# Expert weights fetched with rows p and p + 128 in one partition instead of two neighbouring rows

## The chip, the cores and the metric

The kernel runs on one core of one Trainium2 chip. The metric is the device time of one execution in microseconds (us). A core has five engines with instruction queues of their own: TensorE (PE; its weight loads are listed apart as PEld), VectorE (DVE), ScalarE (ACT), GpSimd (POOL) and SyncE (SP), which here only issues transfers. 16 DMA engines move the data of all queues.

## The reference, cut to what matters

Two transformer blocks over 256 tokens of 1,024 features, in float32. The first mixes tokens and then retrieves single-neuron experts, 128 per token, out of a table of 16,384 rows. The second has a recurrent mixer, an attention and then a mixture of 32 experts, each of which is a 1,024 x 2,048 matrix for gate and up and a 1,024 x 1,024 matrix down:

```python
def expert_block(args):
    tok, e = args
    xb = h[tok]
    gu = xb @ w_gate_up[e] + b_gate_up[e]
    gate = jnp.minimum(gu[:, :D_FF], SWIGLU_LIMIT)
    up = jnp.clip(gu[:, D_FF:], -SWIGLU_LIMIT, SWIGLU_LIMIT)
    act = (up + 1.0) * gate * jax.nn.sigmoid(SWIGLU_ALPHA * gate)
    return act @ w_down[e] + b_down[e]
```

A router picks 4 experts per token. All 32 experts are needed, so 32 x 12.58 MB = 402.65 MB of weights are read once.

## The kernel before

SBUF holds a ring of 12 slots of 1,024 KB (8 KB in each of 128 partitions) and an arena that is laid out anew in each stage.

Stage one, to about 1,060 us. The weights of the dense layers come as a stream of 93 chunks, one slot each (SP, L639). `slot_of` says which slot a chunk takes: the first 48 go round the ring; the q chunks take `Q_SLOTS`, the keys and what follows take the slots of `FREE`, and the remaining seven slots (`G_SLOTS`) hold rows of the table of single-neuron experts, 256 gathers of 128 rows of 8 KB that GpSimd issues (L743). A chunk is issued when TensorE has counted `chunk_done` past the last user of its slot. Work of the second block is woven into the gathers; what is left of it is done after them, to the transposes of the residual at L2235 and the router at L2249.

Stage two, the 32 experts. A weight transfer ("pair") moves 2,048 KB: two k-chunks of 128 rows of `w_gate_up` (four pairs per expert), or four of `w_down` (two pairs). There are nine places: six are two slots of the ring each (`in_ring`), three lie in the arena. Transfer m goes to place m % 9. SP issues the first nine when the last users of their place are through, and each later one when the transfer nine before it is used up (L648, in `pair`). Slots 10 and 11, 5 and 6, 7 and 8, 3 and 4, 0 and 1 are neighbours; place 7 is slots 2 and 9.

With `(p i)` in the source's order, partition p holds rows 2p and 2p + 1 of the 256 rows of the pair. A k-chunk is then the even or the odd rows, so the other operand must have its features in that order too. The kernel gets this by reading every second column in the transposes (`front_turn`, L2310; L2235 for the router's input), by reading every fourth for the input of `w_down` (L2338), and by permuting the matching columns on the host (`paired`).

An expert on TensorE: 64 matmuls of gate and up (L2324), the gathering of the next expert's tokens (L2291), biases (L2302), transposes of the activation (L2338), of the next expert's input (L2310) and of the scatter matrix (L2344), 32 matmuls down (L2355), and 8 that add the result into the residual (L2367). TensorE waits in `pair(q)` for the landing of each weight pair.

Of the kernel before, what the change touches and what calls it, by code (L numbers as in the profile page):

```python
# [14 lines left out]
P = 128  # L15
D = 1024
T = 256
TT = T // P
KD = D // P
CW = 256  # L20
# [23 lines left out]
NE = 32  # L44
# [34 lines left out]
ADA_PARTS = (0, 1, 3, 4, 2, 5)  # L79
N_PARTS = len(ADA_PARTS)  # L80
# [41 lines left out]

Q_SLOTS = (0, 1, 2, 4, 0, 1, 2, 4)
FREE = (0, 1, 2, 4, 3)
G_SLOTS = tuple(sorted(set(range(SLOTS)) - set(FREE)))
GB, NF = len(G_SLOTS), len(FREE)
PICKS = TT * HK
# [130 lines left out]
def build(nc, xd, stream, colsd, matsd, rowsd, badad, expert_uv, w_gate_up, w_down, bias_moe, out):  # L260
    with ExitStack() as ctx:
# [8 lines left out]
        xres = sb("xres", [P, TT, D])  # L270
# [5 lines left out]
        ident = sb("ident", [P, P])  # L276
# [17 lines left out]
        psum = ctx.enter_context(nc.psum_tensor("psum", [P, 8, 512], F32))  # L294
# [121 lines left out]
        xs = area(6144, W2)  # L416
        xT = area(6656, 4, P)
        ag = area(7168, 512)
# [204 lines left out]
        @block.sync  # L623
        def _(sp):
            sp.dma_start(cols[:], colsd).then_inc(loaded_c, 16)
            for tt in range(TT):
                sp.dma_start(xres[:, tt, :], xd[tt * P:(tt + 1) * P, :]).then_inc(loaded_x[tt], 16)
            held = {}
            for n in LOADS:
                if C_MB + N_GATHER <= n < C_MB + N_GATHER + GB:  # L630
                    sp.wait_ge(v_done, PICKS - GB + (n - C_MB - N_GATHER) + 1)
                elif slot_of(n) in held:
                    sp.wait_ge(chunk_done, held[slot_of(n)] + 1)
                if n == C_MB + N_FIRST:
                    sp.wait_ge(v_done, PICKS - LEFT)
                held[slot_of(n)] = n
                kind = STREAM[n][:2]
                width = KD * LAST if kind == ("rw", N_RW - 1) else CHUNK
                sp.dma_start(slot(n)[:, 0:width], stream[ROW[kind], :, 0:width]).then_inc(landed[slot_of(n)], 16)  # L639

            def pair(e, q, at):

                if q < GU_PAIRS:
                    src = w_gate_up[e, q * 2 * P:(q + 1) * 2 * P, :].rearrange("(p i) c -> p i c", i=2)
                else:
                    r = (q - GU_PAIRS) * 4 * P
                    src = w_down[e, r:r + 4 * P, :].rearrange("(p i k) c -> p i (k c)", i=2, k=2)
                sp.dma_start(place(at), src).then_inc(pair_in(at)[0], 16)  # L648


            for m in range(PLACES):
                if m in in_ring:
                    sp.wait_ge(chunk_done, max(n for n in range(C_MOE) if slot_of(n) in in_ring[m]) + 1)
                elif m == 4:
                    sp.wait_ge(pv_mm, TT)
                    sp.wait_ge(yp_mm, TT)
                    sp.wait_ge(fg_mm, 4 * TT)
                elif m == 5:
                    sp.wait_ge(chunk_done, AT["o2", 0, TT - 1] + 1)
                else:  # L660
                    sp.wait_ge(chunk_done, AT["o2", N_O2 - 1, TT - 1] + 1)
                pair(m // E_PAIRS, m % E_PAIRS, m)

            for m in range(PLACES, AHEAD * E_PAIRS):
                sp.wait_ge(chunk_done, C_MOE + (m - PLACES + 1))
                pair(m // E_PAIRS, m % E_PAIRS, m % PLACES)
            with sp.Fori(0, (NE - AHEAD) // ROUND) as i:
                for k in range(ROUND * E_PAIRS):
                    m = AHEAD * E_PAIRS + k
                    sp.wait_ge(chunk_done, i * (ROUND * E_PAIRS) + (C_MOE + m - PLACES + 1))  # L670
                    pair(i * ROUND + m // E_PAIRS, m % E_PAIRS, m % PLACES)

            def experts(p):
                with sp.Fori(0, NE) as e:
                    for q in range(E_PAIRS):
                        sp.wait_ge(chunk_done, (p * NE + e) * E_PAIRS + (C_MOE + q - E_PAIRS + 1))
                        pair(e, q, last_pass_place(q))

            further_passes(sp, experts)
            sp.wait_ge(out_ready, 1)  # L680
            for tt in range(TT):
                sp.dma_start(out[tt * P:(tt + 1) * P, :], xres[:, tt, :]).then_inc(stored, 16)
            sp.wait_ge(stored, 16 * TT)
# [1057 lines left out]
        def _(pe):  # L1741
# [264 lines left out]
            def mixer(tt):  # L2006
# [223 lines left out]
                for m in range(2):  # L2230
                    yield "tn%d" % m
                    pe.wait_ge(xn_ready[3], 2 * tt + m + 1)
                    for k in range(4 * m, 4 * m + 4):
                        at = k // 2 * 2 * P + k % 2
                        last = pe.transpose(psum[:, m, k % 4 * P:(k % 4 + 1) * P], xres[:, tt, at:at + 2 * P - 1:2], ident[:])  # L2235
                    last.then_inc(turned[3], 1)
                if tt:
                    pe.wait_ge(picks_ready, 1)
# [66 lines left out]
            def front_turn(f):  # L2305
                pe.wait_ge(xs_ready, f + 1)
                for j in range(4):

                    at = j // 2 * 2 * P + j % 2
                    last = pe.transpose(psum[:, 3, j * P:(j + 1) * P], xs[:, at:at + 2 * P - 1:2], ident[:])  # L2310
                last.then_inc(xt_mm, 1)

            def expert(it, f, pair):

                pe.wait_ge(xT_ready, f + 1)
                for kt in range(GU_CHUNKS):
                    if kt % 2 == 0:
                        both = pair(kt // 2)
                    w = both[:, kt % 2, :]
                    x = xT[:, kt % 4, CAP * (kt // 4):CAP * (kt // 4) + CAP]  # L2320
                    for gu in range(2):
                        for h in range(2):
                            at = gu * FF + h * 512
                            last = pe.matmul(psum[CAP * h:CAP * h + CAP, gu, :], x, w[:, at:at + 512],  # L2324
                                             start=False, stop=(kt == GU_CHUNKS - 1), skip_group_check=True)
                    if kt % 2 and kt < GU_CHUNKS - 1:
                        last.then_inc(chunk_done, 1)
                last.then_inc(gu_mm, 1)

                pe.wait_ge(sct_ready, it + 1)  # L2330
                front_gather(f + 1, frees=True)
                pe.wait_ge(gu_read, it + 1)
                biases(f + 1)
                pe.wait_ge(act_ready, it + 1)
                pe.wait_ge(acc_done, it * TT + 1)
                for j in range(4):

                    last = pe.transpose(psum[:, 4, j * P:(j + 1) * P], ag[:, j:j + 4 * P - 3:4], ident[:])  # L2338
                last.then_inc(at_mm, 1)
                front_turn(f + 1)  # L2340

                pe.wait_ge(ohw_ready, it + 1)
                for tt in range(TT):
                    last = pe.transpose(psum[:, 2, tt * P:(tt + 1) * P], ohw[:, tt, :], ident[:])  # L2344
                last.then_inc(sct_mm, 1)
                pe.wait_ge(actT_ready, it + 1)
                for q in range(DN_CHUNKS):
                    if q % 2 == 0:
                        both = pair(GU_PAIRS + q // 2)
                    w = both[:, q % 2, :]  # L2350
                    for i in range(2):
                        kt = 2 * q + i
                        a_in = act_t[:, kt % 4, CAP * (kt // 4):CAP * (kt // 4) + CAP]
                        for h in range(2):
                            last = pe.matmul(psum[CAP * h:CAP * h + CAP, 5, :], a_in,  # L2355
                                             w[:, i * D + h * 512:i * D + h * 512 + 512],
                                             start=False, stop=(kt == KD - 1), skip_group_check=True)
                    if q % 2 and q < DN_CHUNKS - 1:
                        last.then_inc(chunk_done, 1)
                last.then_inc(y_mm, 1)  # L2360
                pe.wait_ge(sct_ready, it + 2)
                pe.wait_ge(ye_ready, it + 1)
                pe.wait_ge(xT_ready, f + 2)
                for tt in range(TT):
                    for h in range(2):
                        rows = slice(CAP * h, CAP * h + CAP)
                        last = pe.matmul(psum[:, (6, 3)[tt] + h, :], sct[rows, tt, :], ye[rows, :],  # L2367
                                         start=True, stop=True)
                        if tt == 0 and h == 0:
                            last.then_inc(chunk_done, 1)  # L2370
                    last.then_inc(sum_mm, 1)
# [110 lines left out]
```

## Time and profile before

| | |
|---|---|
| median of 3 runs | 1998.14 us (1997.38 to 2000.53) |
| the profiled execution's own time | 1998.14 us |
| its span, first to last instruction | 1996.4 us |
| TensorE busy | 1733.7 us, 87% |
| moved by DMA | 772.99 MB, mean 387 GB/s |
| weight pairs | 192 of 2,048 KB, issued by SP |
| mean granted TensorE clock | 0.920 |

The time is some 1.7 us longer than the span of the profile. DMA transfers are made of packets; the profile counts them and the bytes of each queue. "Share" is the part of the time in which the 16 engines had a packet in hand; it can go a little over 1 because packets overlap.

### The profile page before, as it was taken

Reading aid. Unit: us, or ns where it says so; the run is one execution under the profiler, and the core shown is the slowest. Engines: PE = TensorE matmul, PEld = TensorE weight load, DVE = VectorE, ACT = ScalarE, POOL = GpSimd, SP = SyncE. Lnnn points to the kernel's source line nnn. Section 1 sums busy time; section 2 is a strip of 40 time slices with the busy share of each in tenths; the row PEclk is TensorE's granted clock in tenths of the full one; section 3 lists DMA queues with packets and bytes.
Section 4 is the critical chain, followed back from the end, with each engine's and each line's share of the span. In section 5 each row is a group of like instructions: output and inputs, shape, how many; then the busy total and the mean of one; then the engine's idle time right before and its main releaser. Section 6 shows DMA issues by size and latency. Waiting matters only on the chain.

```text
span 1996.4 us, 30466 instructions
## 1 busy us (share of the span) xinstructions
PE 1733.7 (87%) x12368; PEld 818.0 (41%) x12368; DVE 932.8 (47%) x2007; ACT 472.3 (24%) x1182; POOL 286.1 (14%) x286
## 2 busy tenths in 40 slices
PE   7999987676679877867878999999999999999997
PEld 6888554111136534415764333333333333333332
DVE  4754878788664756654343223232322233223222
ACT  1111434333344633343211011110111011101101
POOL 1000333344433344440000000000000000000000
PEclk9999998757679988877978999999999999999999
DMA  9991999999999999999517999999999999999997
GB/s 388 381 381 71 383 421 421 420 422 421 421 393 421 391 390 378 420 422 394 216 53 316 426 426 427 427 429 427 428 428 427 429 426 429 427 428 428 426 429 297
DMA packets 82107, 772.99 MB, mean 387 GB/s; under 512 B 9077, under 2 KB 9333, under 8 KB 10201
## 3 DMA queue, kind: packets, MB, share of 16 engines
q1 hardware_dynamic: 44448, 500.50, 59.8%
q0 software_dynamic: 36864, 268.45, 32.9%
q10 hardware_dynamic: 696, 2.66, 0.4%
q8 instruction: 70, 1.15, 0.2%
q14 instruction: 29, 0.23, 0.0%
HBM read 770.53 MB, written 1.05 MB: 386 GB/s over the span
## 4 chain that ended last, share of the span: by engine, by line
PE 58%; DMA 25%; DVE 8%; ACT 4%; issue 4%; POOL 1%; DVEq 0%; SPq 0%; POOLq 0%; ACTq 0%
PE psum L2324 16%; DMA ring<-in_expert_uv,arena 14%; DMA ring<-in_w_gate_up 11%; PE psum L2355 9%; PE psum L1919 7%; PE psum L1771 6%; PE psum L2367 3%; PE psum L2034 2%; PE psum L1876 2%; DVE ring L1318 2%; PE psum L1854 1%; PE psum L1962 1%; PE psum L1839 1%; PE psum L2338 1%; PE psum L2113 1%
## 5 line engine op out<-in xcount | busy, mean ns | idle before, releaser
L1919 PE MATMUL psum<-ring,arena 64*64 64x512 f32 x2048 | 353.9, 777 | 139.6 <-ACT arena L876 135.8
L1318 DVE CUSTOM_DVE_ANT_0 ring<-ring,arena 128x1024 f32<-128x1024 f32 x256 | 311.6, 1224 | 159.2 <-DMA ring<-in_expert_uv,arena 154.7
L743 POOL DMA_INDIRECT ring<-in_expert_uv,arena x256 | 275.9, 1078 | 608.1 <-PE psum L1919 401.8
L2324 PE MATMUL psum<-ring,arena 128*64 128x512 f32 x1552 | 346.6, 597 | 12.4 <-DMA ring<-in_w_gate_up 10.9
L2324 PEld LDWEIGHTS psum<-ring,arena 128*64 128x64 f32 x1552 | 107.8, 137 | 244.3 <-issue 220.3
L1919 PEld LDWEIGHTS psum<-ring,arena 64*64 64x64 f32 x2048 | 66.9, 156 | 343.7 <-ACT arena L876 312.3
L1716 DVE TENSOR_SCALAR arena<-psum 128x512 f32<-128x512 f32 x32 | 22.1, 692 | 381.3 <-PE psum L2324 381.3
L1031 ACT ACTIVATE arena<-arena 128x512 f32<-128x512 f32 x32 | 20.2, 630 | 738.8 <-DVE arena L1716 738.8
L867 ACT ACTIVATE arena<-arena 128x1 f32<-128x1 f32 x256 | 51.6, 202 | 319.8 <-DVE arena L1318 319.0
L2355 PE MATMUL psum<-ring,arena 128*64 128x512 f32 x512 | 114.5, 596 | 0.0
L2355 PE MATMUL psum<-arena 128*64 128x512 f32 x512 | 114.0, 594 | 0.0
L1771 PE MATMUL psum<-arena,ring 128*128 128x256 f32 x512 | 112.3, 381 | 0.0
L2324 PE MATMUL psum<-arena 128*64 128x512 f32 x496 | 110.0, 592 | 0.0
L1725 DVE TENSOR_TENSOR arena<-psum,gates 128x512 f32<-128x512 f32 x32 | 22.1, 691 | 188.0 <-PE psum L2355 188.0
L1771 PEld LDWEIGHTS psum<-arena,ring 128*128 128x128 f32 x512 | 97.4, 191 | 13.5 <-issue 0.4
L1728 DVE TENSOR_TENSOR xres<-xres,psum 128x1024 f32<-128x1024 f32 x64 | 75.3, 1218 | 40.8 <-PE psum L2367 40.8
L876 ACT ACTIVATE arena<-ident,arena 128x64 f32<-128x64 f32 x256 | 89.0, 348 | 8.4
L2367 PE MATMUL psum<-arena 64*128 64x512 f32 x256 | 63.6, 611 | 26.9 <-issue 26.9
L871 ACT ACTIVATE arena<-arena,peer_g 128x1 f32<-128x1 f32 x256 | 75.4, 294 | 8.8
L1876 PEld LDWEIGHTS psum<-arena,ring 128*128 128x128 f32 x512 | 59.4, 191 | 24.2 <-issue 24.2
L1876 PE MATMUL psum<-arena,ring 128*128 128x128 f32 x512 | 65.0, 281 | 0.9 <-ACT arena L776 0.9
L2324 PEld LDWEIGHTS psum<-arena 128*64 128x64 f32 x496 | 35.6, 137 | 70.9 <-issue 66.8
(358 smaller groups left out, 1782.7 us busy)
## 6 DMA issues: line engine op xcount, KB each, us to landing
ring<-in_w_gate_up SPq DMA_DIRECT2D x97, 2048.0 KB, 28.3
ring<-in_stream SPq DMA_DIRECT2D x91, 1024.0 KB, 13.0
arena<-in_w_down SPq DMA_DIRECT2D x32, 2048.0 KB, 29.6
ring<-in_w_down SPq DMA_DIRECT2D x32, 2048.0 KB, 30.8
arena<-in_w_gate_up SPq DMA_DIRECT2D x31, 2048.0 KB, 28.2
ring<-in_expert_uv,arena POOLq DMA_INDIRECT x256
mats<-in_mats ACTq DMA_DIRECT2D x1, 1152.0 KB
xres<-in_x SPq DMA_DIRECT2D x2, 512.0 KB, 4.2
```

Source lines behind the costliest of these rows:

```text
L743: pool.indirect_dma_start(ring[:, G_SLOTS[b], :], None, expert_uv, bass.IndirectOffsetOnAxis(peer_i[:, tt, k:k + 1], 0)).then_inc(row_in[b ...
L867: act.activation(one, one, ACT.Gelu).then_inc(weight_step, 1)
L871: act.activation(peer_w[:, 0, c % 4:c % 4 + 1], one, ACT.Copy, scale=peer_g[:, tt, k:k + 1]).then_inc(weight_step, 1)
L876: act.activation(diag[:, c % 4, :], ident2[:], ACT.Copy, scale=peer_w[:, 0, c % 4:c % 4 + 1]).then_inc(diag_ready, 1)
L1318: dve.tensor_tensor_reduce(u, u, h2[tt], 1.0, 0.0, ALU.mult, ALU.add, peer_h[:, tt, k:k + 1]).then_inc(dot_done, 1)
L1728: dve.tensor_tensor(xres[:, tt, :], xres[:, tt, :], psum[:, (6, 3)[tt]:(8, 5)[tt], :].rearrange("p a c -> p (a c)"), ALU.add).then_inc(acc ...
L1771: last = pe.matmul(psum[:, bank, c * T:(c + 1) * T], wide(n)[:, k, c * P:(c + 1) * P], acts[:, k, :], start=(k == 0), stop=(k == KD - 1))
L1876: last = pe.matmul(psum[:, bank, o:o + P], wide(n)[:, k, cs], h2T[:, k, ts], start=(k == 0), stop=(k == KD - 1), skip_group_check=True)
L1919: last = pe.matmul(psum[o:o + 64, 6 * tt + h, :], diag[rows, c % 4, :], rows_of[b][rows, 1, h * 512:(h + 1) * 512], start=(k == 0), stop=( ...
L2324: last = pe.matmul(psum[CAP * h:CAP * h + CAP, gu, :], x, w[:, at:at + 512], start=False, stop=(kt == GU_CHUNKS - 1), skip_group_check=True)
L2355: last = pe.matmul(psum[CAP * h:CAP * h + CAP, 5, :], a_in, w[:, i * D + h * 512:i * D + h * 512 + 512], start=False, stop=(kt == KD - 1), ...
L2367: last = pe.matmul(psum[:, (6, 3)[tt] + h, :], sct[rows, tt, :], ye[rows, :], start=True, stop=True)
```

## The change

The pair's source is read as `(i p)`: partition p gets rows p and p + 128 of the pair, so each k-chunk is 128 rows that follow one another. The transposes, the input of the router and the host's order of columns follow. `w_down` keeps its inner `k` of two rows together, so L2338 reads with step 2 instead of 4. Slots 2 and 3 change roles in `Q_SLOTS` and `FREE`; by that, place 3 becomes slots 2 and 4, and place 7 slots 3 and 9.

```diff
-Q_SLOTS = (0, 1, 2, 4, 0, 1, 2, 4)
-FREE = (0, 1, 2, 4, 3)
+Q_SLOTS = (0, 1, 3, 4, 0, 1, 3, 4)
+FREE = (0, 1, 3, 4, 2)
...
-                    src = w_gate_up[e, q * 2 * P:(q + 1) * 2 * P, :].rearrange("(p i) c -> p i c", i=2)
+                    src = w_gate_up[e, q * 2 * P:(q + 1) * 2 * P, :].rearrange("(i p) c -> p i c", i=2)
...
-                    src = w_down[e, r:r + 4 * P, :].rearrange("(p i k) c -> p i (k c)", i=2, k=2)
+                    src = w_down[e, r:r + 4 * P, :].rearrange("(i p k) c -> p i (k c)", i=2, k=2)
...
                     for k in range(4 * m, 4 * m + 4):
-                        at = k // 2 * 2 * P + k % 2
-                        last = pe.transpose(psum[:, m, k % 4 * P:(k % 4 + 1) * P], xres[:, tt, at:at + 2 * P - 1:2], ident[:])
+                        last = pe.transpose(psum[:, m, k % 4 * P:(k % 4 + 1) * P], xres[:, tt, k * P:(k + 1) * P], ident[:])
...
                 for j in range(4):
-
-                    at = j // 2 * 2 * P + j % 2
-                    last = pe.transpose(psum[:, 3, j * P:(j + 1) * P], xs[:, at:at + 2 * P - 1:2], ident[:])
+                    last = pe.transpose(psum[:, 3, j * P:(j + 1) * P], xs[:, j * P:(j + 1) * P], ident[:])
...
-                    last = pe.transpose(psum[:, 4, j * P:(j + 1) * P], ag[:, j:j + 4 * P - 3:4], ident[:])
+                    at = j // 2 * 2 * P + j % 2
+                    last = pe.transpose(psum[:, 4, j * P:(j + 1) * P], ag[:, at:at + 2 * P - 1:2], ident[:])
...
-    paired = np.arange(D).reshape(KD // 2, P, 2).transpose(0, 2, 1).reshape(D)
...
-    w_ada = chunks(a["w_ada_2"][0][:, ada_at])
+    w_ada = chunks(a["w_ada_2"][0])
...
-        "norm2_g": a["norm2_g_2"].reshape(-1)[paired], "c": a["c_2"]}
+        "norm2_g": a["norm2_g_2"], "c": a["c_2"]}
...
-    router = a["w_router_2"][0][paired].reshape(KD, P, NE).transpose(1, 0, 2).reshape(P, KD * NE)
+    router = a["w_router_2"][0].reshape(KD, P, NE).transpose(1, 0, 2).reshape(P, KD * NE)
```

## Rows read from the trace of the kernel before

**Rows 1.** The page: the span in 40 equal slices, busy tenths and GB/s.

```profile
PE   7999987676679877867878999999999999999997
...
DMA  9991999999999999999517999999999999999997
GB/s 388 381 381 71 383 421 421 420 422 421 421 393 421 391 390 378 420 422 394 216 53 316 426 426 427 427 429 427 428 428 427 429 426 429 427 428 428 426 429 297
```

**Rows 2.** The page: a DMA queue (packets, MB, share) and issues by tile (KB, us to landing).

```profile
q1 hardware_dynamic: 44448, 500.50, 59.8%
...
ring<-in_w_gate_up SPq DMA_DIRECT2D x97, 2048.0 KB, 28.3
```

**Rows 3.** The chain of waits, experts: start us, us, what.

```profile
1103.62 13.91 PE psum L2324 x64
...
1638.28 3.61 PE psum L2324 x16
...
1694.99 3.61 PE psum L2324 x16
...
1930.38 3.61 PE psum L2324 x16
1934.14 37.16 DMA ring<-in_w_gate_up
1971.34 3.68 PE psum L2324 x16
```

**Rows 4.** Waits from 1,640 to 1,990 us: us in total, times, longest.

```profile
PEld psum L2324 <- DMA ring<-in_w_gate_up: 22.0, 14, 2.0
```

**Rows 5.** Windows: stretch, length, PE, PEld, DVE, ACT, POOL, PEclk, DMA share, GB/s.

```profile
22.00:62.00 40.00, 40.00 (x192) 34.61 (x191) 26.98 (x32) 3.52 (x6) 0.00 (x0) 1.00 1.01 422
...
400.00:590.00 190.00, 129.44 (x632) 27.65 (x632) 143.17 (x366) 77.89 (x242) 77.52 (x75) 0.67 1.01 415
...
560.00:570.00 10.00, 4.34 (x27) 1.01 (x24) 9.86 (x16) 6.48 (x13) 2.17 (x3) 0.61 1.01 421
...
590.00:595.00 5.00, 5.00 (x38) 3.21 (x31) 2.57 (x6) 2.40 (x10) 2.31 (x2) 1.00 1.02 383
...
600.00:605.00 5.00, 5.00 (x46) 3.57 (x44) 1.53 (x4) 0.48 (x1) 1.99 (x2) 1.00 1.02 423
...
917.00:922.00 5.00, 1.21 (x6) 1.22 (x7) 3.96 (x10) 0.20 (x2) 0.00 (x0) 0.50 1.01 428
...
930.00:952.00 22.00, 22.00 (x197) 21.08 (x196) 10.59 (x31) 11.32 (x22) 0.00 (x0) 1.00 1.01 420
...
1070.00:1080.00 10.00, 7.74 (x28) 2.58 (x28) 2.38 (x7) 1.87 (x2) 0.00 (x0) 0.79 0.37 156
...
1090.00:1970.00 880.00, 838.79 (x4136) 291.61 (x4132) 250.54 (x434) 107.23 (x155) 0.00 (x0) 1.00 1.01 427
```

**Rows 6.** Timeline of SP's queue: start us, us, line, operation.

```profile
1079.18 0.33 SPq L648 DMA_DIRECT2D ring<-in_w_gate_up  x1
```

**Rows 7.** DMA view of 1,200 to 1,900 us.

```profile
DMA packets 22602, 299.34 MB, mean 428 GB/s; under 512 B 2284, under 2 KB 2284, under 8 KB 2284
```

**Rows 8.** DMA view of 30 to 55 us.

```profile
DMA packets 1442, 10.53 MB, mean 421 GB/s; under 512 B 158, under 2 KB 158, under 8 KB 158
```

**Rows 9.** Lines L1892, L2310, L2338, L2344: duration ns min/median/max, first and last start.

```profile
L1892 PE MATMUL psum<-ring,arena x56: 275/275/580, 225.8 to 366.4; 128*128 128x128 f32 x56
...
L2310 PEld LDWEIGHTS psum<-ident,arena x132: 195/209/216, 1071.5 to 1978.7; 128*128 128x128 f32 x132
...
L2338 PEld LDWEIGHTS psum<-ident,arena x128: 195/209/222, 1092.3 to 1978.3; 128*128 128x128 f32 x128
...
L2344 PEld LDWEIGHTS psum<-ident,arena x64: 141/147/157, 1093.2 to 1979.0; 128*128 128x128 f32 x64
```

**Rows 10.** Timeline of TensorE, one expert: start us, us, line, operation.

```profile
1317.38 0.74 PE L2338 MATMUL psum<-ident,arena 128*128 128x128 f32 x4 [0.19 <-DVE arena L1722]
...
1318.44 0.38 PE L2344 MATMUL psum<-ident,arena 128*128 128x128 f32 x2
```

More of the change, by code:

```diff
@@ L2433 @@
     w2 = np.concatenate([w2[:, RW:], w2[:, :whole]], axis=1)
-    paired = np.arange(D).reshape(KD // 2, P, 2).transpose(0, 2, 1).reshape(D)
-    ada_at = np.arange(6 * D).reshape(6, D)
-    ada_at[3:5] = ada_at[3:5][:, paired]
-    ada_at = ada_at.reshape(-1)
-    w_ada = chunks(a["w_ada_2"][0][:, ada_at])
+    w_ada = chunks(a["w_ada_2"][0])
     parts = {
@@ L2461 @@
     gup = gup.transpose(1, 0, 2).reshape(P, 2 * W2)
-    router = a["w_router_2"][0][paired].reshape(KD, P, NE).transpose(1, 0, 2).reshape(P, KD * NE)
+    router = a["w_router_2"][0].reshape(KD, P, NE).transpose(1, 0, 2).reshape(P, KD * NE)
     mats = np.concatenate([group, lora, gup, router], axis=1)
     rows = np.concatenate([a["g_ffn"].reshape(-1), a["g_final"].reshape(-1), a["b_router_2"].reshape(-1)])[None]
-    bada = a["b_ada_2"].reshape(-1)[ada_at].reshape(N_PARTS, 4, CW)[list(ADA_PARTS)].transpose(1, 0, 2).reshape(4, N_PARTS * CW)
+    bada = a["b_ada_2"].reshape(N_PARTS, 4, CW)[list(ADA_PARTS)].transpose(1, 0, 2).reshape(4, N_PARTS * CW)
     expert_uv = np.concatenate([a["expert_u"][0], a["expert_v"][0]], axis=1)
```

## The prediction, made before the change was run

> **What bounds the kernel now.** I read the page first. [rows 1] show three stretches: a start with the stream of weights at about 380 GB/s, a middle at about 420, and from slice 23 on (1,098 us) an even 426 to 429 GB/s with all 16 DMA engines busy and TensorE at "9" too. Two engines look full, so busy shares can't say which one sets the end. The change touches how every expert's weights are fetched, 6 for each of 32 experts, 192 transfers of 2,048 KB [rows 2], so the question is whether those transfers are on the path.
>
> The chain of waits answers it [rows 3]. From 1103.62 to 1638.28 it runs through TensorE alone, 19 experts of (1638.28 - 1103.62) / 19 = 28.14 us. Then it changes: between 1694.99 and 1930.38, 8 experts take 29.42 us each, and 37 us of every two are put down to the transfer of gate-up weights. The wait that ends last there is the weights' [rows 4]. A cross-check: an expert is 6 transfers of 2,048 KB = 12.58 MB, and at 427.5 GB/s (windows of 427 and 428 in [rows 5, 7]) that is 29.43 us, the period seen. So the weights need 29.43 us per expert and TensorE 28.14. TensorE eats the lead of nine places at 1.29 us per expert, has eaten it near 1640, and then walks at the transfers' pace. The first 20 experts look bound by TensorE, but the last landing doesn't depend on that: the DMA engines never rest between 1,090 and 1,970 us [rows 5]. The end is set by when that stream starts, its bytes, its rate, and a fixed tail from the landing at 1971.34 (the fourth transfer of the last expert) to the end at 1996.4.
>
> When does the stream start? The first nine transfers go out as places come free and are done by about 1,075 us (DMA share 0.37 in 1,070 to 1,080 [rows 5]). The tenth waits for expert 0 to free a place and is issued at 1079.18 [rows 6]. From there to the landing that counts, transfers 10 to 190 pass: 181 of 2.097 MB, 379.6 MB. At 427.5 GB/s they take 888 us, and 1079.2 + 888 + some 3 to 4 us to begin and to be noticed = 1971, as seen.
>
> **The change part by part.** *(a) Source order of the expert weights, (p i) to (i p).* Before, a partition takes two neighbouring rows, 16 KB in one run. After, it takes rows p and p + 128, two runs of 8 KB that lie 1 MB apart; for w_down likewise, with (k c) still 8 KB. Bytes, transfers, places and waits stay the same in number; packets double. Are packets cut now where a run ends? [rows 7] count them: 299.34 MB in 1,200 to 1,900 are 142.7 transfers; 22,602 packets less 2,284 small ones are 20,318, where 142.7 x 128 = 18,270 packets of 16 KB would do. The surplus of 2,048 is 16 transfers times 128, one transfer in nine. One place of the nine lies in ring slots 2 and 9, which aren't neighbours, so its destination is already in two runs. A cut run does make two packets, and after the change all nine places have them.
>
> What do 8 KB packets cost? The stream of the first stage moves 8 KB per partition in 1,024 KB transfers: 422 GB/s in 22 to 62 us and 420 in 930 to 952 us, at the same DMA share 1.01 [rows 5]; of 1,442 packets in 25 us of it 158 are small, the rest 8 KB [rows 8]. The gathers of 8 KB rows from places all over a table run at 421 GB/s in 560 to 570 us [rows 5], so a far jump of the address between packets costs nothing more. I take 421.5 GB/s. Then 379.6 MB take 900.6 us instead of 888.0: **+12.6 us**. Bounds: at 423 (in 600 to 605 us, gathers and stream together, [rows 5]) +9.4; at 420 +15.8. Nothing hides it, since no gap is left in the stream; the tail starts later by the whole amount. The ninth that is cut already is inside the 427.5.
>
> The Trainium skill, "DMA: Bandwidth & Descriptors", section "Why small descriptors are slow (HBM only)", gives a fixed cost of about 3 cycles beside 32-byte beats. Estimated from that page, an 8 KB packet is 256 + 3 cycles and a 16 KB one 512 + 3, which is 0.6% less rate, and this sum would be +5 us. The trace has 1.4% between its two rates, and the trace's price is used.
>
> *(b) Reads of the transposes.* front_turn (four per expert) and the transposes of xres at L2235 read neighbouring columns instead of every second one; those of ag at L2338 read every second instead of every fourth. In [rows 9] the weight load takes 209 ns median with step 2 (L2310) and with step 4 (L2338), and 147 with step 1 (L2344). So L2338 gains nothing. Four with a step (L2338) span 0.74 us with the pipeline's start, two of L2344 0.38 [rows 10], so four with step 1 should span some 0.60: 0.15 us per group. That makes an expert of TensorE some 0.15 us shorter, covered by the 1.29 us that TensorE is faster than the weights; it only spends the lead a little earlier. Three groups lie on the path before 1079.18 (two at L2235, one at L2310), of which the last two are in the chain without cover: **-0.3 us**, between 0 and -0.5. In the tail the group of L2310 stands beside the copies that L2355 waits for: nothing.
>
> The Trainium skill, "SBUF — State Buffer", in its note on cachelines, puts a step of up to 4 float32 as free. By it (b) would be 0 instead of -0.3; the loads in [rows 9] speak against it, if their 209 against 147 ns comes from the step.
>
> *(c) Slots 2 and 3 change roles.* The same sequence of holders runs through both from the second q chunk on. Only their start differs: the keys wait for modulation chunk 22 instead of 23, and q chunk 2 for 23 instead of 22, both one chunk apart, 2.5 us each way at 421 GB/s. Q chunk 2 is queued behind the keys anyway and so left at the later of both before: 0. The keys are used first at 225.8 us [rows 9], and the stream has run dry before that (71 GB/s in slice 4, 150 to 200 us [rows 1]). Places 3 and 7 of the weights now lie in slots 2, 4 and 3, 9, both in two runs; with (a) the source is cut everyhow, so a place costs nothing more.
> *(d) Order of the columns on the host* (w_ada, router, norm2_g, b_ada): same bytes, same transfers, 0.
>
> Sum: +12.6 - 0.3 = +12.3 us on a span of 1996.4, which gives 2008.7. The profiled execution's time is 1998.14, 1.7 above its span, and it is also the median of the three runs. **2010.4 us.**
>
> **Rivals.** *R1, no cost.* The price of 8 KB packets in the other stages could come from their 1,024 KB transfers or the gather's issue and not from the packet. Then the rate stays 427.5 and only (b) is left: 1997.8. Against it: the gather and SP's stream are issued differently and have one rate. For it: 428 in 917 to 922 [rows 5] shows 8 KB packets at full rate for the first 5 us after a pause. 9%.
> *R2, dearer addresses.* Each engine now alternates between two addresses 1 MB apart, always the same distance, while the gather jumps at random. If all engines meet in the same parts of the memory, the rate falls below both rows. The nearest row of 8 KB packets that is slower under a full share is the gathers' 400 to 590 us at 415: 914.7 us, +26.7 - 0.3, 2024.5; the farthest is 383 in 590 to 595, which would be +103. Its place is (a) alone, and it decides from 418 GB/s down (+20). 8%. The Trainium skill, same DMA page, section "Latency and other measured facts", reports 16 KiB rows at power-of-two pitches slowing from 214 to 207 GB/s at 512 KiB and 164 at 2 MiB. As an estimate by that page a pitch of 1 MiB would cost between 3 and 30%, +27 to over +250 us; here the pitch between partitions is 8 KB, and only two rows of each partition stand 1 MB apart, so no row here shows it.
> *R3, faster.* If two streams 1 MB apart were served faster than one, the end would come earlier, until TensorE binds: expert 30 would begin at 1638.28 + 10 x 28.14 = 1919.7 instead of 1930.38, so with one more expert 11.9 us is all there is, 1985.9, at 27.99 us per expert with (b) a little more. It decides, by the 4 us that count, from 429.5 GB/s on. The windows never pass 428. 3%.
>
> **How the numbers follow.** Forecast 80%, R1 9%, R2 8%, R3 3%. What a measurement here can tell from no change is 0.2%, 4 us. Slower 0.88, same 0.09, faster 0.03. The forecast's own range is 2007 to 2014 (bounds of (a) and (b)); to hold 8 in 10 with part of R1 and R2, and with the three runs' own spread of 3 us, I give 2004 to 2017.
>
> **What would show it.** About 49,300 data packets for the expert weights in place of 27,300, so 66,000 or more on the SP queue where 44,448 were; 421 to 422 GB/s in 1,200 to 1,900 us; a period of 12.58 / 0.4215 = 29.85 us in the last experts; the first wait for weights near expert 15 instead of 20, since the lead of 20 x 1.29 = 26 us goes at 29.85 - 27.99 = 1.86 us per expert; L2310 and L2235 with weight loads near 147 ns and L2338 still at 209. Start of the stream at 1078.9. The prediction is wrong if the rate stays at 427 (R1), falls under 418 (R2), or if anything before 1,079 us moves by over 1 us.

## The result, and the profile after

The changed kernel takes 2009.08 us in the median, the kernel before, run beside it, 1997.47 us: a ratio of 1.0057, 95% interval 1.004 to 1.0074. That is slower by 0.57%, 11.6 us, and the interval stays clear of no change. The forecast was 2010.4 us, +12.3. The profiled execution of the changed kernel took 2010.61 us with a span of 2008.9. One execution of the changed kernel took 2582.35 us at a mean granted TensorE clock of 0.638, where all others had 0.92 to 0.93; the ratio leaves it out.

First the page of the kernel after: the GB/s of the slices that answer to [rows 1], and the SP queue that answers to [rows 2].

```profile
GB/s 388 377 377 75 385 421 421 421 421 421 421 391 420 389 404 381 421 420 384 169 52 360 421 422 421 422 422 422 422 422 422 422 422 422 422 422 422 422 422 301
...
q1 hardware_dynamic: 66336, 500.50, 60.3%
```

The slices before the experts show the same pattern as before. From slice 23 on, where [rows 1] had 426 to 429 GB/s, stand 421 and 422, as flat as before. The bytes of the queue are the same; its packets rose from 44,448 to 66,336, by 21,888 = 171 x 128. These are the 171 transfers whose 128 runs of 16 KB were whole.

The windows of the kernel after (stretch, length, five engines, TensorE's clock, DMA share, GB/s), and the counts of packets of 1,200 to 1,900 us, answer to [rows 5, 7].

```profile
22.00:62.00 40.00, 40.00 (x191) 34.61 (x190) 26.99 (x32) 3.51 (x6) 0.00 (x0) 1.00 1.01 422
...
1200.00:1900.00 700.00, 659.66 (x3244) 226.16 (x3246) 196.28 (x339) 83.84 (x122) 0.00 (x0) 1.00 1.01 422
```

```profile
DMA packets 38306, 295.34 MB, mean 422 GB/s; under 512 B 2256, under 2 KB 2256, under 8 KB 2256
```

The stream of the first stage, which the change doesn't touch, has 422 GB/s as before, and the experts' stream now has the same 422. The DMA share stayed 1.01: the engines are as full and carry less.

The chain of waits of the kernel after (start us, us, what), against [rows 3]:

```profile
1104.73 13.91 PE psum L2321 x64
...
1526.83 3.61 PE psum L2321 x16
1530.59 8.30 SPq L648
...
1655.77 3.68 PE psum L2321 x16
...
1894.32 3.68 PE psum L2321 x16
...
1983.79 3.68 PE psum L2321 x16
```

L2321 is the L2324 of before. TensorE now has used up its lead at 1526.83 instead of 1638.28, 15 experts after 1104.73 where it took 19. From then on an expert takes (1894.32 - 1655.77) / 8 = 29.82 us instead of 29.42. The last wait for gate-up weights ends at 1983.79 instead of 1971.34. New in this chain are steps of SP's own queue, 4.4 to 10.6 us long, about one or two transfers. The line that issues the weights shows what they are (duration ns min/median/max):

```profile
L648 SPq DMA_DIRECT2D ring<-in_w_gate_up x97: 367/2442/10559, 956.0 to 1951.0; - x97
```

Before, the same instruction took 0.33 us in the median and at most 0.67 (0.86 for any weight transfer). SP now stands in many of its issues. The first 62 after 1,100 us are not held, though, and the rate is the lower one already:

```profile
L648 SPq DMA_DIRECT2D ring<-in_w_gate_up x32: 372/373/373, 1108.5 to 1389.9; - x32
```

```profile
1100.00:1390.00 290.00, 278.83 (x1378) 97.10 (x1376) 85.00 (x148) 34.56 (x50) 0.00 (x0) 1.00 1.01 422
```

So the held issues are not what lowers the rate to 422 GB/s. Whether they cost anything beside it is a question for the experiments.

### The profile page after: what moved, and what is told of

Read it like the earlier page. It is cut to its first block, busy times and chain, and to the rows that moved or that the text cites. A ratio compares the mean times of both kernels' runs of the same rounds, so it can differ in the third digit from the quotient of the medians.

```text
span 2008.9 us, 30466 instructions
## 1 busy us (share of the span) xinstructions
PE 1730.5 (86%) x12368; PEld 810.9 (40%) x12368; DVE 933.1 (46%) x2007; ACT 471.7 (23%) x1182; POOL 285.3 (14%) x286
## 3 DMA queue, kind: packets, MB, share of 16 engines
q1 hardware_dynamic: 66336, 500.50, 60.3%
## 4 chain that ended last, share of the span: by engine, by line
PE 51%; DMA 24%; SPq 8%; DVE 8%; ACT 4%; issue 4%; POOL 0%; ACTq 0%; DVEq 0%; POOLq 0%
DMA ring<-in_expert_uv,arena 15%; PE psum L2321 13%; DMA ring<-in_w_gate_up 10%; SPq L648 8%; PE psum L2353 7%; PE psum L1919 6%; PE psum L1771 6%; PE psum L2034 2%; PE psum L1876 2%; PE psum L2365 2%; DVE ring L1318 2%; PE psum L1854 1%; PE psum L1962 1%; PE psum L1839 1%; PE psum L2227 1%
## 5 line engine op out<-in xcount | busy, mean ns | idle before, releaser
L2321 PE MATMUL psum<-ring,arena 128*64 128x512 f32 x1552 | 347.6, 598 | 20.9 <-DMA ring<-in_w_gate_up 19.3
L2321 PEld LDWEIGHTS psum<-ring,arena 128*64 128x64 f32 x1552 | 107.1, 137 | 255.2 <-issue 216.5
L2321 PE MATMUL psum<-arena 128*64 128x512 f32 x496 | 110.8, 594 | 0.0
L1771 PEld LDWEIGHTS psum<-arena,ring 128*128 128x128 f32 x512 | 97.5, 191 | 13.6 <-issue 0.4
L1876 PEld LDWEIGHTS psum<-arena,ring 128*128 128x128 f32 x512 | 63.8, 203 | 25.8 <-issue 25.8
L1876 PE MATMUL psum<-arena,ring 128*128 128x128 f32 x512 | 69.6, 293 | 0.9 <-ACT arena L776 0.9
L2321 PEld LDWEIGHTS psum<-arena 128*64 128x64 f32 x496 | 34.8, 137 | 72.9 <-issue 65.4
```

The lines of the kernel that those rows point to most:

```text
L1771: last = pe.matmul(psum[:, bank, c * T:(c + 1) * T], wide(n)[:, k, c * P:(c + 1) * P], acts[:, k, :], start=(k == 0), stop=(k == KD - 1))
L1876: last = pe.matmul(psum[:, bank, o:o + P], wide(n)[:, k, cs], h2T[:, k, ts], start=(k == 0), stop=(k == KD - 1), skip_group_check=True)
```

## The experiments

The first stage is not equally long in each execution. The tenth weight transfer, from which the stream never rests, was issued between 1075.35 and 1084.84 us in the profiled executions, also where that stage's code is the same. So beside each median stands a second reading, the span less the moment of that tenth issue, "from the stream's start": 1996.4 - 1079.18 = 917.2 us before, and 2008.9 - 1080.28 = 928.6 after, +11.4. It rests on one profiled execution per kernel; the four kernels that cut every transfer in two agree in it within 0.8 us. All ratios are to the kernel before.

| kernel | median us | ratio (95%) | from the stream's start | against 917.2 | GB/s 1,200 to 1,900 |
|---|---|---|---|---|---|
| after | 2009.08 | 1.0057 (1.004 to 1.0074) | 928.6 | +11.4 | 422 |
| order only | 2010.04 | 1.0063 (1.0049 to 1.0076) | 928.9 | +11.7 | 422 |
| near, 8 KB | 2008.91 | 1.0058 (1.0044 to 1.0072) | 929.3 | +12.1 | 422 |
| 4 MB apart | 2007.67 | 1.0057 (1.0041 to 1.0072) | 928.6 | +11.4 | 422 |
| near, 4 KB | 2038.58 | 1.0207 (1.0192 to 1.0223) | 956.1 | +38.9 | 410 |
| all but the order | 2000.06 | 1.0011 (1.0002 to 1.0021) | 918.2 | +1.0 | 427 |
| down kept | 2004.39 | 1.0042 (1.0028 to 1.0055) | 925.1 | +7.9 | 424 |
| neighbours | 1997.33 | 0.9995 (0.9986 to 1.0003) | 915.8 | -1.4 | 428 |
| less weights, before | 1984.87 | 0.993 (0.9915 to 0.9945) | 904.1 | -13.1 | 410 |
| less weights, after | 1983.50 | 0.9927 (0.9909 to 0.9944) | 904.1 | -13.1 | 410 |

**The order alone, and all but the order.** Two kernels that share the change between them.

```diff
-                    src = w_gate_up[e, q * 2 * P:(q + 1) * 2 * P, :].rearrange("(p i) c -> p i c", i=2)
+                    src = w_gate_up[e, q * 2 * P:(q + 1) * 2 * P, :].rearrange("(i p) c -> p i c", i=2)
...
-                    src = w_down[e, r:r + 4 * P, :].rearrange("(p i k) c -> p i (k c)", i=2, k=2)
+                    src = w_down[e, r:r + 4 * P, :].rearrange("(i p k) c -> p i (k c)", i=2, k=2)
```

> The kernel before with the weights' source order (i p) alone, transposes, host order and slots as before (the features meet the wrong rows, so the values differ; the work is the same). Packets theory (a transfer cut into 256 packets of 8 KB takes 0.075 us longer than one of 128 packets of 16 KB): 161 more cut transfers, +12 us, a ratio of 1.006, 421 to 422 GB/s in the expert stage. Rival (part of the 11.6 us comes from the slots or the transposes): under +9 us.

The other is the changed kernel with these two lines as before.

> The changed kernel with the source order (p i) back, so everything else of the change alone (values differ, work the same). Two of nine places are cut instead of one: 21 more cut transfers x 0.075 = +1.6 us. Prediction's step (b): -0.3 us from three shorter groups of transposes before the stream starts, nothing in the experts. Sum +1.3, within 0.2% of before. Rival (the later start of the stream in the changed kernel, 1080.28 against 1079.18, belongs to the change): the first L648 issue after e0 at 1080 or later again, and +2.5 us.

The order alone costs 13 us in the median and 11.7 from the stream's start: all of the change's cost. The rest costs 2 us in the median, interval 0.4 to 4, and 1.0 from the stream's start. Its stream shows the second place in two runs:

```profile
DMA packets 24548, 298.78 MB, mean 427 GB/s; under 512 B 2280, under 2 KB 2280, under 8 KB 2280
```

24,548 less 2,280 small ones are 22,268 packets where 298.78 MB in 16 KB make 18,236: 4,032 more, 31.5 transfers x 128, two of nine (142.5 x 2/9 = 31.7), where [rows 7] had one. Its stream started at 1084.84, later than any other, and its median is 2.3 us above that of before: nearly the sign of the rival that was named for this run (1080 or later, and +2.5 us). But the three other kernels with the changed first stage started at 1077.23, 1078.64 and 1080.28. With the first stage of the kernel before it was 1075.35, 1077.77, 1078.48, 1079.18 and 1081.15. The two sets overlap, so the 1.1 us by which the changed kernel's stream started later can't be given to the change; whether a part of it belongs there stays open.

**Packets or addresses.** Twice the packets and a distance of 1 MB came together in the change. Two kernels part them. In the first the source stays one run, and the two halves change places in the destination; in the second the two rows of a partition are 4 MB apart in the gate-up weights, two thirds of the bytes, and 1 MB apart in the down weights.

```diff
-                sp.dma_start(place(at), src).then_inc(pair_in(at)[0], 16)
+                sp.dma_start(place(at)[:, ::-1, :], src).then_inc(pair_in(at)[0], 16)
```

> The kernel before with the two 8 KB halves of each partition's run exchanged in the destination (values differ, work the same). The source stays one run of 16 KB, its two packets are neighbours in HBM. Packets theory: +12 us and 421 to 422 GB/s as with rows 1 MB apart. Address theory (the distance of 1 MB between an engine's packets costs): no change, 1997 us and 427 GB/s.

```diff
-                    src = w_gate_up[e, q * 2 * P:(q + 1) * 2 * P, :].rearrange("(p i) c -> p i c", i=2)
+                    src = w_gate_up[e].rearrange("(i q p) c -> q p i c", i=2, q=GU_PAIRS)[q]
...
-                    src = w_down[e, r:r + 4 * P, :].rearrange("(p i k) c -> p i (k c)", i=2, k=2)
+                    src = w_down[e, r:r + 4 * P, :].rearrange("(i p k) c -> p i (k c)", i=2, k=2)
```

> The kernel before with (i p) for the down weights and, for gate and up, the two rows of a partition 4 MB apart instead of 1 MB (chunks q and q + 4 in one transfer; values differ, work the same). Packets theory: as with 1 MB, +12 us, 421 to 422 GB/s. Address theory: another rate than at 1 MB, by at least 1%, so another 9 us or more.

The windows of 1,200 to 1,900 us, first the near kernel's, then the far one's:

```profile
1200.00:1900.00 700.00, 659.62 (x3247) 227.17 (x3242) 196.97 (x340) 84.28 (x123) 0.00 (x0) 1.00 1.01 422
```

```profile
1200.00:1900.00 700.00, 659.98 (x3250) 227.87 (x3240) 196.50 (x340) 85.63 (x124) 0.00 (x0) 1.00 1.01 422
```

Neighbours in HBM, 1 MB apart or 4 MB apart: 422 GB/s each time, and 12.1, 11.7 and 11.4 us from the stream's start. The address theory (R2) falls for these distances. It also makes no difference which side cuts the run.

**The price of a packet, and SP's queue.** If a packet has a fixed price, 4 KB pieces must cost three times what 8 KB pieces cost: 384 packets more per transfer instead of 128. This kernel stands on the one with renamed slots below, so that all runs are whole to begin with.

```diff
-                sp.dma_start(place(at), src).then_inc(pair_in(at)[0], 16)
+                src = src.rearrange("p i (h c) -> p (i h) c", h=2)
+                sp.dma_start(place(at).rearrange("p i (h c) -> p (i h) c", h=2)[:, ::-1, :], src).then_inc(pair_in(at)[0], 16)
```

> Ring slots renamed so that all places are neighbours, and each partition's 16 KB laid down as four pieces of 4 KB in reversed order (values differ, work the same): 512 packets per transfer, no jump in the source. Packets theory with a fixed price per packet: 128 more packets cost 0.075 to 0.078 us, so 384 more cost 0.23, 5.13 us per transfer, 409 GB/s, 30.8 us per expert and +40 us, some 2038. SP is held in its issue longer than in the changed kernel, and no time comes from that. Address theory: no change. Rival (SP's held queue is what costs): more than +60 us, with gaps between transfers, DMA share under 0.98.

Its window and its issues of gate-up weights (over 1,200 to 1,900 us it moved 72,173 packets, all but one under 8 KB):

```profile
1200.00:1900.00 700.00, 641.82 (x3144) 219.37 (x3142) 190.29 (x328) 83.01 (x120) 0.00 (x0) 1.00 1.03 410
```

```profile
L650 SPq DMA_DIRECT2D ring<-in_w_gate_up x97: 539/4716/10012, 955.2 to 1986.9; - x97
```

2038.58 us, where 2038 was expected, and 410 GB/s where 409 was. Against the kernel with whole runs it is 956.1 - 915.8 = 40.3 us for 384 more packets in each of 181 transfers. 16 engines share them, so 24 each, and a packet costs 40.3 / (181 x 24) = 9.3 ns of an engine. The change itself gives 11.4 / (161 x 8) = 8.9 ns. One price per packet fits both sizes, within what a single profiled execution of each can tell.

SP stands in nearly every issue here, 4.7 us in the median, and the chain from 1,900 us on gives it more than half of the time:

```profile
by line: SPq L650 56.3%; DMA ring<-in_w_gate_up 16.9%; PE psum L2357 7.2%; issue 4.0%; PE psum L2326 2.6%; PE psum L2369 1.6%; DVE xres L1730 0.9%; PE psum L2340 0.5%; DVE arena L1721 0.5%; DVE arena L1724 0.5%; DVE arena L1718 0.5%; DVE ar
```

That line would send a reader to SP. But from 1,085 to 1,165 us none of this kernel's issues is held (0.54 us each), and the rate is 410 GB/s already; later, with nearly every issue held, it is 410 still. The rival for this run wanted more than 60 us and a DMA share under 0.98, and got 41.6 and 1.03. So the held issue costs nothing here, and the time fits without any term for it. That SP is held because its queue is full is the likely reading; the traces show how long it stands, not what it waits for.

**Half of it back.** The down weights go back to (p i k), with the transpose of the activation again at step 4.

```diff
-                    src = w_down[e, r:r + 4 * P, :].rearrange("(i p k) c -> p i (k c)", i=2, k=2)
+                    src = w_down[e, r:r + 4 * P, :].rearrange("(p i k) c -> p i (k c)", i=2, k=2)
...
-                    at = j // 2 * 2 * P + j % 2
-                    last = pe.transpose(psum[:, 4, j * P:(j + 1) * P], ag[:, at:at + 2 * P - 1:2], ident[:])
+                    last = pe.transpose(psum[:, 4, j * P:(j + 1) * P], ag[:, j:j + 4 * P - 3:4], ident[:])
```

> The changed kernel with w_down fetched as before, (p i k), and L2336 reading with step 4 again; computes the reference. Packets theory: two thirds of the transfers are cut by their source and two ninths of the rest by their place: (128 + 64 x 2/9) - 21 = 121 more cut than before, +9 us, a third of the change's cost given back (3 us less than the changed kernel), 423.5 GB/s. If the cost were per expert or per wait and not per packet, it stays at +12.

7.9 us from the stream's start and 424 GB/s, expected 9 and 423.5. A third of the cost is given back with a third of the cut transfers. The queue's packets, 59,424, show 117 more cut transfers than before and not the 121 that were expected: the two places in two runs take a down transfer only once in 18 transfers. By the medians 6.6 us of the 11.6 are left. The step of 4 in the transpose takes nothing in return.

**All places neighbours.** The reverse of the change, on the kernel before: its one place in two runs becomes whole.

```diff
-Q_SLOTS = (0, 1, 2, 4, 0, 1, 2, 4)
-FREE = (0, 1, 2, 4, 3)
-G_SLOTS = tuple(sorted(set(range(SLOTS)) - set(FREE)))
+PHYS = (0, 1, 2, 4, 5, 6, 7, 8, 9, 3, 10, 11)
+Q_SLOTS = (0, 1, 2, 5, 0, 1, 2, 5)
+FREE = (0, 1, 2, 5, 4)
+G_SLOTS = (6, 7, 8, 9, 3, 10, 11)
...
-        return n % SLOTS
+        return PHYS[n % SLOTS]
```

> The kernel before with the ring slots renamed so that place 7 lies in neighbours too; computes the reference. Packets theory: the 21 cut transfers become whole, -1.6 us, 428.2 GB/s, all of the stream's packets of experts 16 KB (128 per transfer). Cost: five more runs of the modulation sums, 40 more VectorE operations in the first stage, nothing to +2 us. Rival: the first stage loses more than the experts gain.

```profile
DMA packets 20592, 299.92 MB, mean 428 GB/s; under 512 B 2287, under 2 KB 2287, under 8 KB 2287
```

20,592 less 2,287 are 18,305 packets, 299.92 MB in 16 KB and none more. From the stream's start it is 1.4 us shorter (expected 1.6), but the median is 1997.33 and the ratio's interval, 0.9986 to 1.0003, holds 1. It doesn't beat the kernel before by anything that can be told. Whether the first stage pays for the 1.4 us stays open: its stream started at 1084.00, and that of the 4 KB kernel, with the same first stage, at 1079.63.

**Where the stream has room.** The last two leave out half of the last transfer of each expert, once before and once after the change. TensorE's work stays; the first nine transfers stay whole.

```diff
-            def pair(e, q, at):
+            def pair(e, q, at, whole=False):
...
-                sp.dma_start(place(at), src).then_inc(pair_in(at)[0], 16)
+                n = 1 if q == E_PAIRS - 1 and not whole else 2
+                sp.dma_start(place(at)[:, 0:n, :], src[:, 0:n, :]).then_inc(pair_in(at)[0], 16)
...
-                pair(m // E_PAIRS, m % E_PAIRS, m)
+                pair(m // E_PAIRS, m % E_PAIRS, m, True)
```

> The kernel before, with the second half of the last transfer of each expert left out (1,024 KB instead of 2,048, from the tenth transfer on; the last matmuls use what lies in the place, so values differ). Weights then need 5.5 x 4.906 = 27.0 us per expert, less than TensorE's 28.14. Theory (the weights' stream sets the end, TensorE is 11.9 us behind it): 28.14 us per expert to the end, no wait for weights, 11.9 us less than before, a ratio of 0.994. If the end were TensorE's already: no change.

> The changed kernel with the same half left out: 5.5 x 4.97 = 27.3 us of weights per expert, still under TensorE's 28.14. Theory: the cut packets are covered now, so it takes as long as e8_less_before, 11.9 us less than before. Step (b) of the prediction (TensorE 0.15 us shorter per expert): 31 x 0.15 = 4.6 us less than e8_less_before; if the transposes lie beside the copy that the down matmuls wait for: equal to it within 1 us. Rival (the change costs something else than stream time): 11 us more than e8_less_before.

The chain of the first, then of the second:

```profile
1105.60 13.91 PE psum L2325 x64
...
1949.87 13.91 PE psum L2325 x64
```

```profile
1103.08 13.91 PE psum L2322 x64
...
1947.34 13.91 PE psum L2322 x64
```

(1949.87 - 1105.60) / 30 and (1947.34 - 1103.08) / 30 are both 28.14 us per expert, from the second to the last, with no wait for weights. Both need 904.1 us from the stream's start. With room in the stream the cut packets cost nothing, and the shorter transposes gain nothing either. The window of the first shows a trap:

```profile
1200.00:1900.00 700.00, 674.49 (x3335) 236.15 (x3333) 202.49 (x350) 86.41 (x125) 0.00 (x0) 1.00 1.00 410
```

Here TensorE sets the pace and no transfer is waited for, and still the DMA share is 1.00. A full share alone doesn't say that the stream is the bound.

## Why the prediction was right, point by point

**What bounds.** The prediction saw that TensorE alone makes up the chain of the first 20 experts, and held all the same that the stream of weights sets the end since its DMA engines never rest. That reason alone wouldn't carry, as the share of 1.00 in the kernel with less to fetch shows; what carried was the check of the period, 29.43 us by bytes and rate against 29.42 seen. With less to fetch, both kernels fall to TensorE's 28.14 us per expert and become equal, so the cost of the change is time of the stream; no other part of it shows. The floor under R3 was given as 11.9 us; it measured 13.1 from the stream's start. The last expert begins 11.9 us earlier, and it had also stood 1.1 us before its fourth transfer.

**(a) the packets, +12.6.** Measured: 11.4 to 12.1 from the stream's start, in four kernels. The rate came out at 422 instead of 421.5, the period at 29.82 instead of 29.85. That the one already cut place shows in the count of packets was the key: it said that a cut run makes two packets, and two kernels with two and with no cut places confirm it. The price was taken from another stage with 8 KB packets, and it held. The Trainium skill, "DMA: Bandwidth & Descriptors", section "Why small descriptors are slow (HBM only)", states a fixed overhead of about 3 cycles per packet, from which the prediction worked out its other estimate of +5 us. The same page's section "Specifications" gives 435 GB/s over 16 ports of 32 bytes at 850 MHz; a cycle is then 1.18 ns and 3 cycles are 3.5 ns, as an estimate by that page. The runs here show 8.9 to 9.4 ns (11.4 to 12.1 us over 161 x 8 packets, and the 4 KB kernel), and the measurement decides.

**(b) the transposes, -0.3, and 0.15 us shorter experts.** The weight loads came out nearly as read: 140 to 141 ns with step 1 where 147 was said, 209 with step 2. On the line of `front_turn` only the step changed, so the 209 did come from the step.

```profile
L2307 PEld LDWEIGHTS psum<-ident,arena x132: 138/141/157, 1072.7 to 1991.2; 128*128 128x128 f32 x132
...
L2336 PEld LDWEIGHTS psum<-ident,arena x128: 194/209/223, 1093.4 to 1990.7; 128*128 128x128 f32 x128
```

But the step that said what follows from them failed. An expert stays at 28.14 us, not 27.99. The prediction saw for the tail that the group stands beside the copy that the down matmuls wait for, and forgot it for the 31 experts ahead. The first weight load of the down matmuls shows it, before and after (the bracket is the idle time ahead of it and what ended that):

```profile
1318.80 0.20 PEld L2355 LDWEIGHTS psum<-ring,arena 128*64 128x64 f32 x4 [0.21 <-ACT arena L1034]
```

```profile
1319.90 0.20 PEld L2353 LDWEIGHTS psum<-ring,arena 128*64 128x64 f32 x4 [0.26 <-ACT arena L1034]
```

It waits for ScalarE's copy (L1034) both times, and 0.05 us longer after the change. The size was off too: behind the group of L2338 the four of `front_turn` span 0.64 us before and 0.60 after, so 0.04 where 0.15 was said. The prediction had taken 0.74 for four with a step from L2338, which stands first and has the pipeline's start in it. As for the three groups before the stream, in the timelines they are 0.63, 0.75 and 0.75 us before and 0.60, 0.66 and 0.65 after, so 0.1 each for the last two, the ones that count, where 0.15 was said. An effect of that size is lost in a stage whose end varies by 6 to 8 us with the same code, and the -0.3 stays unproven.

**(c) the slots, 0, and (d), 0.** A price was denied to (c) because (a) cuts every source anyway. That holds for the change. By itself (c) would cost some: the kernel with all but the order has 21 more cut transfers and takes 1.0 us more from the stream's start, where the price of a packet gives 1.5.

**The rivals.** R1 (no cost) falls with the order-only kernel. R2 (dearer addresses) falls with the near and the far one. R3 (faster) needed 429.5 GB/s, and no kernel's window of the experts passed 428. What the prediction did not see is SP: it said nothing of an issue that takes 2.4 us and more. That this costs nothing was luck for the number; the stretches without a held issue and the 4 KB kernel had to show it.

**The start of the stream.** 1078.9 was forecast, and the profiled execution had 1080.28, 1.1 us later than before. A move of over 1 us there was one of the prediction's own signs of being wrong. The starts of the other kernels scatter by more than that, so it decides nothing; but the profiled span grew by 12.5 us, 11.4 in the stream and 1.1 ahead of it, and that this lies so near to 12.3 is luck in part.

## What to carry to other kernels

When a stream of transfers sets the end, its price is bytes plus packets. In these kernels, with runs of 4 to 16 KB, a new packet begins wherever the run of either side ends, and a prettier order on the compute side that halves the run is paid in full. Count the packets in the DMA view against bytes / run: it shows which buffers are cut already, and at what size the next change will cut. If the chain runs through a compute engine for most of a stage, look whether the last landing depends on it; a lead that is eaten slowly hides the real bound.

## What the runs showed of the hardware

A packet from HBM to SBUF costs an engine about 9 ns beside its bytes: 8.9 to 9.4 between 16 and 8 KB, 9.3 between 16 and 4 KB, and about the same whether the source (+11.4 and +11.7 us) or the destination (+12.1) ends the run. The distance of the two runs in HBM, 0, 1 or 4 MB, made no difference (422 GB/s each time).

SP's issue of a 2,048 KB transfer takes 0.33 us with 128 packets, 0.37 with 256 (0.54 where the destination cuts them) and 0.54 with 512, as long as it isn't held. Held, a transfer of 256 packets lands 32 to 33 us after its issue, 6.5 transfers of 4.97 us; one of 512 packets 23.6 us after it, 4.6 transfers of 5.12 us. In the kernel whose places are all neighbours, with 128 packets per transfer, no issue took over 0.44 us, and landings of up to 39.9 us, eight transfers, occurred. So smaller packets shorten how far ahead SP gets. Here that cost nothing. What the limit is stays open: 6.5 x 256 and 4.6 x 512 are some 1,660 and 2,360 packets, not one number.
